# A weight tile's high part against both parts of x in one 512-column matmul

## The reference

```
h = rmsnorm(x) @ w_in            # 2048 -> z, xbc, dt, q, k, v, qi, ki, wi
y = [ssd_chunked(...), dsa_attention(...)]
x = x + y @ w_out                # 2048 -> 2048
x = x + square(relu(rmsnorm(x) @ w_up)) @ w_down      # 2048 -> 8192 -> 2048
# second layer: compressed/selected/window attention and a gated delta rule,
h = rms_norm(x) @ w_in_2
x = x + (sigmoid(g_a) * (a @ w_pa) + sigmoid(g_b) * (b @ w_pb)) @ w_o
x = x + square(relu(rms_norm(x) @ w_up_2)) @ w_down_2
x = rms_norm(x)
```

## Time and profile before

| | |
|---|---|
| median of 3 runs | 3017.13 us |
| the profiled execution | 3020.07 us, its span 3018.1 us |
| mean granted TensorE clock | 0.967 |
| PE busy | 2871.0 us, 95% of the span, 22598 matmuls |
| DVE busy | 1679.2 us, 56% |
| ACT busy | 1270.9 us, 42% |
| weights read | 482.80 MB moved, 160 GB/s over the span |

### The profile page before, as it was taken

One profiled execution on the slowest core, in us unless ns is written; L12 is line 12 of the kernel. 1 busy time (PEld: TensorE's weight loads), 2 busy tenths in 40 slices (PEclk: granted clock), 3 DMA queues, 4 the chain that ended last, 5 costly groups with the idle time before them and its releaser, 6 DMA issues.

```text
span 3018.1 us, 50882 instructions
## 1 busy us (share of the span) xinstructions
PE 2871.0 (95%) x22598; PEld 2801.0 (93%) x22598; DVE 1679.2 (56%) x2039; ACT 1270.9 (42%) x1574; POOL 35.4 (1%) x36
## 2 busy tenths in 40 slices
PE   7998998999999999899888999999999999999998
PEld 6888998999999999899887988999989999999998
DVE  4477675555545555545556757654555555455554
ACT  4445453434434344345444334334434344343442
POOL 0000001000000000000000000000000000000000
PEclk9899999999999999989888999999999999999999
DMA  5343434555555555536222323345544555555553
GB/s 197 112 180 126 167 123 145 182 182 182 182 182 184 185 184 177 195 142 249 98 84 83 114 85 126 125 155 182 173 163 154 183 180 188 186 185 182 182 182 112
DMA packets 66467, 482.80 MB, mean 160 GB/s; under 512 B 7399, under 2 KB 7527, under 8 KB 9032
## 3 DMA queue, kind: packets, MB, share of 16 engines
q1 hardware_dynamic: 64944, 468.74, 43.8%
q0 software_dynamic: 928, 9.70, 0.9%
q10 hardware_dynamic: 376, 1.11, 0.1%
HBM read 473.23 MB, written 6.29 MB: 159 GB/s over the span
## 4 chain that ended last, share of the span: by engine, by line
PE 86%; DVE 9%; ACT 3%; issue 1%; DMA 0%; DVEq 0%; ACTq 0%
PE bank L419 25%; PE bank L420 25%; PE bank L421 25%; DVE arena L1199 1%; DVE w_lo L992 1%; PE bank L426 1%; PE bank L428 1%; PE bank L427 1%; DVE arena L1509 1%; DVE arena L1039 1%; ACT w_hi L1661 1%; DVE h L1043 1%; PE bank L839 1%; ACT h L1706 1%; PE bank L893 1%
## 5 line engine op out<-in xcount | busy, mean ns | idle before, releaser
L992 DVE TENSOR_TENSOR w_lo<-weight_ring,w_hi 128x1024 fp32r<-128x1024 f32 x886 | 1081.4, 1231 | 933.8 <-ACT w_hi L1661 932.6
L1661 ACT CAST w_hi<-weight_ring 128x1024 fp32r<-128x1024 f32 x886 | 922.1, 1046 | 926.4 <-PE bank L421 883.7
L419 PE MATMUL bank<-h,w_hi 128*128 128x256 f32 x4240 | 1240.5, 293 | 51.5 <-DVE h L1043 33.7
L420 PE MATMUL bank<-h,w_hi 128*128 128x256 f32 x4240 | 1218.6, 287 | 0.0
L421 PE MATMUL bank<-h,w_lo 128*128 128x256 f32 x4240 | 1217.4, 287 | 0.0
L419 PEld LDWEIGHTS bank<-h,w_hi 128*128 128x128 f32 x4240 | 833.5, 197 | 70.7 <-issue 43.9
L420 PEld LDWEIGHTS bank<-h,w_hi 128*128 128x128 f32 x4240 | 833.9, 197 | 4.8 <-issue 4.6
L421 PEld LDWEIGHTS bank<-h,w_lo 128*128 128x128 f32 x4240 | 832.9, 196 | 0.0
L419 PE MATMUL bank<-mix,w_hi 128*128 128x256 f32 x2560 | 728.6, 285 | 5.3 <-DVE w_lo L992 5.3
L420 PE MATMUL bank<-mix,w_hi 128*128 128x256 f32 x2560 | 725.7, 283 | 0.0
L421 PE MATMUL bank<-mix,w_lo 128*128 128x256 f32 x2560 | 725.6, 283 | 0.0
(11 more groups left out here) (319 smaller groups left out, 1590.9 us busy)
## 6 DMA issues: line engine op xcount, KB each, us to landing
weight_ring<-in_w_up SPq DMA_DIRECT2D x128, 1024.0 KB, 4.8
weight_ring<-in_w_down SPq DMA_DIRECT2D x128, 1024.0 KB, 4.8
weight_ring<-in_w_merge SPq DMA_DIRECT2D x32, 1024.0 KB, 4.8
weight_ring<-in_w_gdn SPq DMA_DIRECT2D x24, 1024.0 KB, 4.8
weight_ring<-in_w_papb SPq DMA_DIRECT2D x16, 1024.0 KB, 4.8
weight_ring<-in_w_o SPq DMA_DIRECT2D x16, 1024.0 KB, 4.7
weight_ring<-in_w_xbc SPq DMA_DIRECT2D x12, 1024.0 KB, 4.8
weight_ring<-in_w_qi SPq DMA_DIRECT2D x8, 1024.0 KB, 9.4
```

Of the source, the lines that this page charges most:

```text
L419: e.matmul(out, hi, x[:, 0, at:at + S], start=first, stop=False)
L420: e.matmul(out, hi, x[:, 1, at:at + S], start=False, stop=False)
L992: e.tensor_tensor(w_lo[:, i, :], ring[:, p % PIECES, half * UNIT:(half + 1) * UNIT], w_hi[:, i, :].bitcast(F32), ALU.subtract).then_inc(un ...
L1661: e.copy(w_hi[:, i, :], ring[:, p % PIECES, half * UNIT:(half + 1) * UNIT]).then_inc(unit_hi, 1)
```

## The change

For one weight tile, W_hi now meets both parts of x in a single matmul of 512 moving columns (256 of x_hi, then 256 of x_lo, taken from the two halves of `hn` or `mix`), and writes all 512 columns of a bank. W_lo meets x_hi in a matmul of 256 columns, into the bank's first half. `products_of_two` takes two weight tiles at a time: both long products, then both short ones. The sum of the two halves of the bank is the result, so a bank now holds one output tile, and every one must be emptied by two engines in turn or by two instructions: ACT copies ("lifts") the second half to SBUF, then DVE adds the first half to it (`add_half`); for the residual DVE adds both halves, one after the other. What was applied on the way out of PSUM (Relu, Silu, Sigmoid, the head norms, the taps, the merge's multiplication) now works on the sum in SBUF; Relu moves into DVE's squaring instruction (max with 0, times itself).

The diff, cut to its core:

```diff
-STAGES = dict(qi=(5, 16), dtwi=(2, 2), ki=(1, 2), q=(4, 16), k=(2, 8), v=(2, 8), xbc=(6, 24), z=(4, 16),
-              out_att=(8, 16), out_ssd=(8, 16), mlp=(65, 256), kv=(5, 16), gab=(2, 2), nq_vsvw=(6, 40), gdn0=(6, 24),
...
+STAGES = dict(qi=(8, 16), dtwi=(2, 2), ki=(1, 2), q=(8, 16), k=(4, 8), v=(2, 8), xbc=(12, 24), z=(8, 16),
+              out_att=(16, 16), out_ssd=(16, 16), mlp=(128, 256), kv=(8, 16), gab=(2, 2), nq_vsvw=(10, 40),
...
-            def products(out, unit_at, o, n, x, at, first, last):
+            def products(bank, unit_at, o, n, x, at, first, last):
 
                 hi, lo = w_hi[:, unit_at % UNITS, o:o + n], w_lo[:, unit_at % UNITS, o:o + n]
-                e.matmul(out, hi, x[:, 0, at:at + S], start=first, stop=False)
-                e.matmul(out, hi, x[:, 1, at:at + S], start=False, stop=False)
-                return e.matmul(out, lo, x[:, 0, at:at + S], start=False, stop=last)
+                e.matmul(bank[:, :], hi, x[:, :, at:at + S], start=first, stop=False)
+                return e.matmul(bank[:, 0:S], lo, x[:, 0, at:at + S], start=False, stop=last)
+
+            def products_of_two(bank, unit_at, o, x, at, first, last):
+
+                for j in range(2):
+                    e.matmul(bank[:, :], w_hi[:, unit_at % UNITS, o + j * P:o + (j + 1) * P],
+                             x[:, :, at + j * S:at + (j + 1) * S], start=first and j == 0, stop=False)
+                for j in range(2):
+                    done = e.matmul(bank[:, 0:S], w_lo[:, unit_at % UNITS, o + j * P:o + (j + 1) * P],
+                                    x[:, 0, at + j * S:at + (j + 1) * S], start=False, stop=last and j == 1)
+                return done
...
# DVE
+            def add_half(dst, bank, read):
+
+                e.wait_ge(lifted, LIFTS[use])
+                e.tensor_tensor(dst, dst, bank[:, 0:S], ALU.add).then_inc(read, 1)
...
-            def residual(s, bank, read):
-                e.tensor_tensor(pair(xT, s), pair(xT, s), bank[:, :], ALU.add).then_inc(read, 1)
+            def residual(t, bank, read):
+                nonlocal n_res
+                e.tensor_tensor(tile(xT, t), tile(xT, t), bank[:, 0:S], ALU.add).then_inc(res_half, 1)
+                n_res += 1
+                e.wait_ge(res_half, n_res)
+                e.tensor_tensor(tile(xT, t), tile(xT, t), bank[:, S:2 * S], ALU.add).then_inc(read, 1)
...
-                e.tensor_tensor(buf, buf, buf, ALU.mult).then_inc(up_squared, 1)
...
+                add_half(tile(buf, t % 2), psum[use % 3], bank_read[use % 3])
+                if t % 2:
+                    bank_done(e, use - 1)
+                    bank_done(e, use)
+                    e.scalar_tensor_tensor(out=buf, in0=buf, scalar=0.0, in1=buf, op0=ALU.max,
+                                           op1=ALU.mult).then_inc(up_squared, 1)
...
# ACT
+            def lift(dst):
+
+                e.wait_ge(unit_used, unit)
+                e.copy(dst, psum[use % 3][:, S:2 * S]).then_inc(lifted, 1)
...
-                    e.activation(buf, psum[use % 3][:, :], ACT.Relu).then_inc(bank_read[use % 3], 1)
-                    use += 1
...
+                lift(tile(buf, t % 2))
+                use += 1
...
# PE, ACT and DVE: column_pair makes two units more ahead
-                split_to(unit + UNITS)
+                split_to(unit + UNITS + 2)
```

More of the change, by code:

```diff
@@ L433, in bank_free, with column @@
                 return psum[use % 3]
-            def column(out, x, first, k_tiles, ready=None):
+            def column(bank, x, first, k_tiles, ready=None):
                 nonlocal unit
-                for k in range(k_tiles):
+                for k in range(0, k_tiles, 2):
                     if k % UNIT_K == 0:
@@ L450, in project @@
                 nonlocal use
[L451 to L456, removed]
+                for t in range(tiles):
+                    yield from column(bank_free(), x, first, k_tiles, None if t else ready)
                     use += 1
@@ L1180, in _, with conv, evacuate @@
             n_conv = 0
-            def conv(name, tiles, acc, first, with_bias=None):
-                def evacuate(s, bank, read):
+            def conv(dst, name, tiles, acc, first, with_bias=None):
+                def evacuate(i, bank, read):
                     nonlocal n_conv
[L1186 to L1205, removed]
@@ new lines, in evacuate @@
+                    t, src, a, b = first + i, tile(dst, i), acc[:, (i % 2) * S:(i % 2 + 1) * S], 4 * n_conv
+                    add_half(src, bank, read)
+                    if n_conv >= 2:
+                        e.wait_ge(conv_silu_done, n_conv - 1)
+                    bank_done(e, use)
+                    if with_bias:
+                        e.tensor_scalar(a, src, vec(name, 3 * tiles + t), vec(with_bias, t), ALU.mult,
+                                        ALU.add).then_inc(conv_taps, 1)
+                    else:
+                        e.tensor_scalar(a, src, vec(name, 3 * tiles + t), None, ALU.mult).then_inc(conv_taps, 1)
@@ L1785, in scoring @@
             def scoring():
-                yield from rounds(4)
+                yield from rounds(5)
                 for n in range(2 * QI_T):
@@ L1955, in _ @@
             norm(2, sq_2, root_2[:, 0:S])
-            def evacuate_kv(s, bank, read):
-                e.wait_ge(unit_used, unit)
-                e.copy(pair(kcvc, s + 1) if s < 1 else pair(kskw, s - 1), bank[:, :]).then_inc(read, 1)
             e.wait_ge(x_saved, 16)
-            column_pair(pair(kcvc, 0), ACT.Copy)
-            drain(project(3, 4, evacuate_kv))
+            column_pair(kcvc)
+            drain(project(6, 2, arena[:, X_AT + 10 * S:]))
             drain(project_tokens(2))
@@ L2007, in some_units, with nq_tile @@
                     unit += 1
-            def evacuate_nq(s):
+            def nq_tile(t):
                 nonlocal use
-                e.wait_ge(unit_used, unit)
-                e.copy(pair(nqT, s), psum[use % 3][:, :]).then_inc(bank_read[use % 3], 1)
+                lift(tile(nqT, t))
                 use += 1
```

402 lines of the change are left out of this document (221 added, 181 removed).

## The result

The changed kernel takes 2917.14 us (median of 4 runs, 2915.40 to 2918.69) against 3017.31 us before: ratio 0.9667, interval [0.9650, 0.9684], 100 us faster. I had forecast 2954 us, range 2935 to 2990. The direction was right, and the gain was 1.6 times as large as forecast, beyond the range's lower end.

What follows compares the result with a forecast made beforehand. PE, busy 95% of the span, was taken as the bound, paced by matmul starts. Terms -67.7 - 20.0 + 10 + 8 + 4 + 2 = -63.7 us gave a median of 2954 us, range 2935 to 2990.

Steps and rivals of the forecast that it cites:

- 77.7 us gained on PE: PE, all 6800 weight tiles: 87.7 us from merged matmuls, less 10 lost in stages beside attention, state-space part and delta rule.
- 14 given back: Added DVE additions and lifts in the open: 8 us in mixed stages, 4 in `out_att`, 2 at stages' ends.
- The surplus of 13.3 ns: PE at full clock: each matmul takes 13.3 ns beyond its columns, whatever its length; merging saves one per weight tile.
- taken off 10: Mixed stages: half of their 20.0 us matmul gain counted as lost, since before a wait a faster PE only waits longer.
- the taps and the gate's multiplication: On reading SBUF in place of PSUM: these keep their sizes, at no cost.
- The clock: PE's mean granted clock, 0.967, used to scale the matmuls' gain from 90.7 to 87.7 us.
- The rivals: Five alternatives, 2929 to 3034 us: gain fully kept, partly or wholly given back, or mostly absent; chances 0.04 to 0.12.
- B: Nothing given back: DVE adds while it now waits for `w_hi`, chains keep their pace; 2929 us, chance 0.07.

Runs made afterwards that it cites:

- a_three: The changed kernel with each long product issued as two matmuls of 256 columns, one into each half of the bank: 2986.11 us.
- b_both: The kernel before with two edits: splitting two units more ahead behind the paired tiles, and Silu two rounds later: 2985.31 us.
- a_small_adds: The changed kernel with its added additions on 8 columns in place of 256, so the projections' sums are left out: 2903.86 us.
- b_ahead: The kernel before with one edit: ACT and DVE split two units more ahead around the paired first tiles: 2997.60 us.
- a_one_run: The changed kernel with the long product's moving operand as one run of 512 columns of x's high part: 2916.84 us.

## Why the prediction was wrong

The sum was 77.7 us gained on PE (87.7 less 10), 14 given back, and nothing else: 63.7. By the runs it is 69 us from the merged matmuls (a_three), 1 given back net (a_three against b_both) and 32.5 from two edits beside them (b_both): 100.5.

**The matmuls: right in mechanism, a little too high.** The surplus of 13.3 ns was read from streams of one length. The pair takes 348.3 ns and not 346.7, which leaves 11.7 of the 13.3 ns, 78 us over 6800 tiles scaled by the clock of 0.977. Of these a_three shows 69 arriving, 9 less, where I had taken off 10. The total surplus was nearly right and its place was not: it is 19.8 ns on a long product and 8.5 on a short one, not 13.3 on each.

**The additions: right by one run, 13 us too high by another.** 14 us forecast, 13.3 for the additions' columns in a_small_adds. `out_att` grew by 1.9 us and `out_ssd` by 0.7; DVE is at 86% in `out_att`. But the whole new way out of PSUM costs 1 us net, since `gdn0` to `gz1` gained 12 us by it. No rival had a gain there, and its cause stays open.

**The step that failed is the list of what the change does beside matmuls and additions.** The working priced "the taps and the gate's multiplication keep their sizes and only read SBUF in place of PSUM, at no cost", and looked at sizes only. It did not ask where the Silu that follows the taps stands in ACT's queue. Before, ACT waited 92.1 us behind the taps, with the exponentials and copies of the chains behind it. Now the Silu is issued one tile later. By the runs a later Silu is worth 11.6 us in the kernel before; in the changed one it is worth 26.2, part of which only offsets waits that the change itself would bring. The taps' wait was in the trace; I never followed it back to the Silu.

**The second is an edit left out of the sum.** The diff shows `split_to(unit + UNITS + 2)`, and the prediction never mentions it. It removes 14.5 us of PE's waits for `w_lo` and is worth 20.4 us before and 26.6 in the changed kernel. The wait of 5.3 us in the earlier trace rows is another one, in `merge0`, and the edit does not touch it (b_ahead still has it). The 14.5 us stood as a term of their own in the trace's groups of line 419, on the row of `h`.

**The clock.** I held it at 0.967. Both edits shorten stops of PE, and the stretches behind them run at the upper level more: 0.84 to 0.89 in `gdn0` by the Silu edit alone. So the removed waits for `w_lo` paid more than their length: 14.5 us of waits gave 20.4.

The rivals were all about giving back. None said that more could come than the matmuls have, which is what happened; B, with nothing given back, ended at 2929 us and was the nearest, but not by its mechanism: the additions' columns alone were 13.3 us in the open.

## What to carry to other kernels

Price every line of a diff, the moved ones before the resized ones: for each instruction that waits, name what stands behind it on its engine before and after. Where a wait of TensorE goes, look at the clock behind it as well. A term's size can be right, as the additions' was, and the sum wrong by the term that is missing.

## What the runs showed of the hardware

- Long (512 columns) and short (256) products with a new 128x128 load for each, at the full clock: two and two 348.3 ns a tile, four and four 350.9, in turn either 353.5 or 346.7. What sets the pace of the last was not found. Alone, each length had 13.3 ns over its columns; in these mixtures a short product took 114.6 to 119.6 ns.
- The moving operand may lie in two runs of 256 columns at no cost: 348.3 ns a tile with it (the change) and without (a_one_run).
- At the lower clock (1.2 GHz) there is no surplus per matmul: 213 ns for 256 columns, and in the changed kernel 427 for a long and 213 for a short product. So a tile takes 640 ns there in either kernel. 32 columns with a new load also take 213 ns at that level, and 111 at the upper one.
